# One 512-column matmul over both parts of x in the first layers of three feed-forward blocks, and two pieces of side work moved in a transformer kernel on Trainium2

## The chip, the cores and the metric

The kernel runs on one core of one Trainium2 chip. TensorE (PE in the profile) multiplies, VectorE (DVE), ScalarE (ACT) and GpSimd (POOL) do the element-wise work, SyncE (SP) issues the weight DMAs. The metric is the device time of one execution in microseconds (us). Before the change three runs gave 1234.70, 1237.61 and 1238.38 us, median 1237.61 us.

## The reference

A sequence of 256 tokens with 1024 features goes through two transformer layers and then a third, hybrid block. Everything is float32. Cut to the parts that the change touches:

```python
def sq_relu_mlp(xn, w1, w2):                      # twice, w1: 1024 x 4096
    return jnp.square(jax.nn.relu(xn @ w1)) @ w2

# layer 1: dilated attention; q and k of three groups get rotary tables
q = apply_rope(hcat[:, :, :, 0], cos_f, sin_f)    # [x1*c - x2*s, x2*c + x1*s]
k = apply_rope(hcat[:, :, :, 1], cos_f, sin_f)

# third block: recurrent branch, then a gated feed-forward
xa = causal_dwconv(xa, lru_conv_w[l], lru_conv_b[l])
r = sigmoid(einsum("bshi,hij->bshj", xh, w_a) + b_a)   # i likewise with w_x
g = causal_dwconv(h @ w_ffn_gate[l], ffn_conv_w[l], ffn_conv_b[l])   # 1024 x 3072, 3 taps
x = x + (jax.nn.gelu(g) * (h @ w_ffn_up[l])) @ w_ffn_down[l]
```

## The kernel before

**Products of split operands.** Each float32 weight and activation is held as a high part and a low part (high is the value rounded to TensorE's fp32r format, low the rest). A product is the sum of three matmuls: high by high, low weight by high activation, high weight by low activation. For x the parts are XH and XL, one 128x256 tile for each of 8 chunks of features.

**Weights.** They come as 192 slabs of 1 MB (128 partitions x 2048 numbers), in one fixed order, through five buffers `raw`. ScalarE writes the high part `whi` (three buffers, function `high`, L1118), VectorE subtracts it and writes the low part `wlo` (function `low`, L1558); for some slabs, the gate slabs of the last feed-forward among them, GpSimd does that (L2273). Both are called two slabs ahead of the slab that TensorE works on (`ahead`). `whi` of a slab waits until TensorE has finished the slab three before it.

**A slab of a first layer.** `features` makes 256 output features of 256 tokens: two halves of 128 features (m), 8 chunks, three matmuls of 256 columns each, 48 in all, into the two halves of one PSUM bank. Its order is chunk by chunk, so it needs `wlo` at its second matmul. `features_low_last` (L550) does all 32 matmuls with `whi` first and the 16 with `wlo` behind them. `tokens` and `by_tokens` make token-major values with 256 or 512 moving columns.

**Order.** Nothing is scheduled at run time: the program of each engine is written out by hand as five functions, one for each engine, and semaphores order them against each other. An engine whose next instruction waits stands still, with all that is behind it.

**The two squared-ReLU blocks (`mlp`).** 16 slabs of W1, then 16 of W2. For each W1 slab ScalarE applies Relu from PSUM into TA (L1222), VectorE squares into TB (L1717), ScalarE rounds TB into HH (L1227), VectorE writes the rest into HL (L1722). Two TA and two TB buffers alternate.

**The gated feed-forward.** 12 pairs of slabs, gate and up. For pair j VectorE scales the gate product out of PSUM into `gv` (memory SN, L2180), applies the three taps (L2186, L2192) into TA, ScalarE applies Gelu (L1516), VectorE multiplies with the up product from PSUM into TB (L2200), ScalarE rounds into HH (L1501), VectorE writes HL (L2206).

**Slabs of the dilated attention.** q and k slabs are rotated: ScalarE copies the product into TA (L1376), four DMAs on its own queue (L1382) bring its 32-row groups swapped into TB, GpSimd multiplies that with the sine (L2339), VectorE multiplies the product with the cosine (L1940) and adds the swapped half (L1920, function `rotate`). Ten slabs (EARLY) stand ahead of the attention, the first six of them q and k. The copy of slab k waits until the sum of slab k-2 is done.

**Recurrent gates.** In the third block's 12 input slabs (`IN2`) VectorE makes a causal convolution of four chunks (`conv`, L2039 and L2043), one behind each of slabs 1 to 4. `lru_gate` multiplies them with small per-head matrices (L994) and ScalarE applies Sigmoid (L1413); slabs 6 and 7 are the attention values.

## Time and profile before

| what | value |
|---|---|
| median of 3 runs | 1237.61 us |
| the profiled execution: its time / its span | 1235.95 / 1234.0 us |
| PE busy | 1218.7 us (99%), 8673 matmuls |
| DVE, ACT, POOL busy | 800.3, 631.4, 206.5 us (65%, 51%, 17%) |
| chain that ended last | PE 89%, DVE 6%, ACT 2% |
| matmuls with x: XH by wlo, XH by whi, XL by whi | 1256 of 256 columns each on line 536 |

The profiled execution took 1235.95 us, of which 1234.0 us are the span shown. The engine lines give busy time; a matmul's own duration (284 ns for 256 columns) holds its way through the array, which overlaps the next one, so the distance from start to start is what counts. The chain is followed back from the last instruction to what released it.

### The profile page before, as it was taken

Reading aid. Unit: us, or ns where it says so; the run is one execution under the profiler, and the core shown is the slowest. Engines: PE = TensorE matmul, PEld = TensorE weight load, DVE = VectorE, ACT = ScalarE, POOL = GpSimd, SP = SyncE. Lnnn points to the kernel's source line nnn. Section 1 sums busy time; section 2 is a strip of 40 time slices with the busy share of each in tenths; the row PEclk is TensorE's granted clock in tenths of the full one; section 3 lists DMA queues with packets and bytes.
Section 4 is the critical chain, followed back from the end, with each engine's and each line's share of the span. In section 5 each row is a group of like instructions: output and inputs, shape, how many; then the busy total and the mean of one; then the engine's idle time right before and its main releaser. Section 6 shows DMA issues by size and latency. Waiting matters only on the chain.

```text
span 1234.0 us, 20616 instructions
## 1 busy us (share of the span) xinstructions
PE 1218.7 (99%) x8673; PEld 1118.9 (91%) x8673; DVE 800.3 (65%) x1071; ACT 631.4 (51%) x785; POOL 206.5 (17%) x160
## 2 busy tenths in 40 slices
PE   9999999999999999999999999998999999999998
PEld 8988999988899989999999988897978899999986
DVE  7778666644475665676876754586975477656643
ACT  5574455534454454445655543455576646444442
POOL 2500010000010201210310000010010695443100
PEclk9999999999999999999999999999999999999999
DMA  9733466555566555654355556554554455555551
GB/s 250 243 103 108 138 183 188 173 203 182 194 212 211 176 179 163 190 186 147 103 165 178 182 194 201 175 185 138 184 163 165 139 190 185 188 171 173 199 182 62
DMA packets 162075, 214.32 MB, mean 174 GB/s; under 512 B 5259, under 2 KB 117198, under 8 KB 161982
## 3 DMA queue, kind: packets, MB, share of 16 engines
q1 hardware_dynamic: 156574, 205.11, 51.6%
q10 hardware_dynamic: 5216, 7.42, 2.1%
q8 instruction: 69, 1.13, 0.4%
q0 software_dynamic: 192, 0.46, 0.2%
q14 instruction: 24, 0.20, 0.0%
HBM read 205.63 MB, written 1.05 MB: 167 GB/s over the span
## 4 chain that ended last, share of the span: by engine, by line
PE 89%; DVE 6%; ACT 2%; DMA 1%; issue 1%; SPq 0%; ACTq 0%; POOL 0%; DVEq 0%
PE ps L536 77%; PE ps L705 3%; PE ps L608 3%; PE ps L742 2%; PE ps L713 2%; DVE wlo L1558 2%; DMA raw<-in_ev_w_in_dram 1%; ACT whi L1118 1%; DVE XT L1691 0%; DVE XL L1596 0%; DVE BIG L2043 0%; DMA TB<-TA 0%; ACTq L1382 0%; DVE RS L1591 0%; PE ps L878 0%
## 5 line engine op out<-in xcount | busy, mean ns | idle before, releaser
L1558 DVE TENSOR_TENSOR wlo<-raw,whi 128x2048 fp32r<-128x2048 f32 (+1 forms) x167 | 385.8, 2311 | 224.2 <-ACT whi L1118 224.0
L1118 ACT ACTIVATE whi<-raw 128x2048 fp32r<-128x2048 f32 x188 | 357.8, 1906 | 196.0 <-PE ps L536 179.8
L536 PE MATMUL ps<-XH,wlo 128*128 128x256 f32 x1256 | 349.5, 284 | 2.4 <-DVE wlo L1558 2.2
L536 PE MATMUL ps<-XH,whi 128*128 128x256 f32 x1256 | 351.3, 285 | 0.0
L536 PE MATMUL ps<-XL,whi 128*128 128x256 f32 x1256 | 349.2, 283 | 0.0
L536 PEld LDWEIGHTS ps<-XH,wlo 128*128 128x128 f32 x1256 | 238.6, 192 | 3.1 <-DVE wlo L1558 3.1
L536 PEld LDWEIGHTS ps<-XH,whi 128*128 128x128 f32 x1256 | 238.6, 192 | 0.2
L536 PEld LDWEIGHTS ps<-XL,whi 128*128 128x128 f32 x1256 | 238.5, 192 | 0.0
L536 PE MATMUL ps<-whi,HL 128*128 128x512 f32 (+1 forms) x416 | 148.7, 373 | 0.0
L536 PE MATMUL ps<-whi,HH 128*128 128x512 f32 x384 | 147.2, 390 | 0.0
L536 PE MATMUL ps<-wlo,HH 128*128 128x512 f32 x368 | 143.2, 389 | 0.0
L2273 POOL TENSOR_TENSOR wlo<-raw,whi 128x512 fp32r<-128x512 f32 x88 | 115.3, 1343 | 145.3 <-ACT whi L1118 145.2
L536 PE MATMUL ps<-whi,XH 128*128 128x512 f32 (+1 forms) x288 | 98.2, 349 | 0.0
L2339 POOL TENSOR_TENSOR TB<-TB,BIG 128x512 f32<-128x512 f32 x24 | 36.4, 1516 | 366.7 <-DMA TB<-TA 366.7
L536 PE MATMUL ps<-wlo,XH 128*128 128x512 f32 (+1 forms) x288 | 96.4, 343 | 0.0
L536 PE MATMUL ps<-whi,XL 128*128 128x512 f32 (+1 forms) x288 | 96.3, 342 | 0.0
L536 PEld LDWEIGHTS ps<-whi,HL 128*128 128x128 f32 x416 | 76.0, 188 | 13.5
L1180 ACT ACTIVATE SN<-SN,stat 128x512 f32<-128x512 f32 (+2 forms) x64 | 38.3, 598 | 96.4 <-DVE stat L1630 93.9
L536 PEld LDWEIGHTS ps<-whi,HH 128*128 128x128 f32 x384 | 71.9, 188 | 14.7
L536 PEld LDWEIGHTS ps<-wlo,HH 128*128 128x128 f32 x368 | 69.1, 188 | 14.5
L536 PEld LDWEIGHTS ps<-whi,XH 128*128 128x128 f32 x288 | 53.6, 190 | 6.9 <-issue 1.1
L536 PEld LDWEIGHTS ps<-wlo,XH 128*128 128x128 f32 x288 | 53.6, 189 | 6.5
(271 smaller groups left out, 1758.3 us busy)
## 6 DMA issues: line engine op xcount, KB each, us to landing
raw<-in_mlp_w_dram SPq DMA_DIRECT2D x64, 1024.0 KB, 5.3
raw<-in_od_w_in_dram SPq DMA_DIRECT2D x36, 1024.0 KB, 5.4
raw<-in_w_in_dram SPq DMA_DIRECT2D x24, 1024.0 KB, 5.1
raw<-in_w_ffn_gate_dram SPq DMA_DIRECT2D x12, 1024.0 KB, 5.2
raw<-in_w_ffn_up_dram SPq DMA_DIRECT2D x12, 1024.0 KB, 5.1
raw<-in_w_ffn_down_dram SPq DMA_DIRECT2D x12, 1024.0 KB, 5.0
TB<-TA ACTq DMA_DIRECT2D x96, 64.0 KB, 4.1
raw<-in_w_branch_dram SPq DMA_DIRECT2D x6, 1024.0 KB, 5.0
```

What stands on the lines that cost most here:

```text
L536: m = pe.matmul(to, l[c][a], r[c][b], start=first and k == 0, stop=last and k == 3 * n - 1)
L608: i = pe.matmul(b[n][:, m * S:m * S + S], h[a], x[c][z], start=m == c == a == z == 0, stop=m == 1 and c == 7 and z == 1)
L705: m = pe.matmul(banks[u][:, lo:hi], l, r, start=start, stop=stop)
L713: m = pe.transpose(b[:, to:to + P], SN[:, u % 3, of:of + P], ident[:, :])
L742: m = pe.matmul(b[p0:p0 + n, a:z], v, PT[:, u % 3, lo:hi], start=start, stop=stop)
L1118: act.activation(whi_of(n), raw_of(n), ACT.Copy, scale=1.0).then_inc(*tell(s_whi, ("whi", n)))
L1180: m = act.activation(SN[:, u % 3, lo:hi], src[:, lo:hi], ACT.Exp, bias=stat[:, u % 3, k:k + 1], scale=-1.0 if biased else 1.0, accum_out=s ...
L1558: dve.tensor_tensor(wlo_of(n), raw_of(n), f32(whi_of(n)), ALU.subtract).then_inc(*tell(s_wlo, ("wlo", n)))
L2273: m = pool.tensor_tensor(lo[:, v], r[:, v], f32(hi[:, v]), ALU.subtract)
L2339: pool.tensor_tensor(z, z, twice(RP[:, S:512]), ALU.mult).then_inc(*tell(s_pool, ("sine", k)))
```

## The change

Three things are edited.

**1. Both parts of x beside each other.** XH and XL become two halves of one tile XHL, 512 columns for each chunk. A new function `beside` replaces `features` for slabs 2 to 15 of both squared-ReLU blocks and slabs 2 to 23 of the gated feed-forward, 14 + 14 + 22 = 50 slabs. Per half it does 8 matmuls of `whi` by 512 columns and then 8 of `wlo` by the 256 high columns, into a bank of its own: columns 0 to 255 hold high x and low weight sums, 256 to 511 the part of low x. ScalarE copies the second half of each bank to SBUF (`copies`), VectorE adds the first half to it (`added`); then the ReLU and the square are one VectorE instruction, and the gated feed-forward scales and multiplies from SBUF. In `mlp` VectorE's `low` stands behind the square instead of ahead of it.

```diff
+            def beside(n, x, between=None):
+                for m in range(2):
+                    b = bank(("beside", n, m))
+                    w = w_ready(n, 8, m * P, P)
+                    for c in range(8):
...
+                        pe.matmul(b[:, :], w[c][0], XHL[:, c, :], start=c == 0, stop=False)
+                    for c in range(8):
+                        once.wait_ge(*at(w[c][3]))
+                        i = pe.matmul(b[:, 0:S], w[c][1], x[c][0], start=False, stop=c == 7)
...
-                    features(W1[layer] + j, x_ready(f"mlp{layer}"))
+                    beside(W1[layer] + j, x_ready(f"mlp{layer}"))
...
-                features(n, x)
+                beside(n, x)
...
+            def copies(n, to, *ready):
+                for m in range(2):
+                    b = take(("beside", n, m), ready)
+                    act.activation(to[:, m * S:m * S + S], b[:, S:2 * S], ACT.Copy, scale=1.0)...
...
+            def added(n, to, copy):
+                for m in range(2):
+                    b = take(("beside", n, m), [("copy", n, m)])
+                    v = slice(m * S, m * S + S)
+                    dve.tensor_tensor(to[:, v], b[:, 0:S], copy[:, v], ALU.add)...
+                once.wait_ge(*at(("taken", "beside", n, 1)))
...
+                        added(W1[layer] + j, a, z)
+                        dve.scalar_tensor_tensor(out=z, in0=a, scalar=0.0, in1=a, op0=ALU.max, op1=ALU.mult)...
...
+                if j:
+                    copies(FF + 2 * j, TA[j % 2], *([("ffn z", j - 2)] if j > 1 else []))
                 once.wait_ge(*at(("ffn conv", j)))
                 act.activation(TA[j % 2][:, :], TA[j % 2][:, :], ACT.Gelu_apprx_tanh)...
+                if j:
+                    copies(FF + 2 * j + 1, TB[j % 2], *([("hlo", 2, j - 2)] if j > 1 else []))
```

**2. Swapped halves' sums moved back.** Among the first ten dilated slabs the sum of the swapped half stands two slabs behind its own, behind the `low` of that slab, and slabs 4 and 5 also use `features_low_last`.

```diff
-                        (features_low_last if i < 4 else features)(n, x)
+                        (features_low_last if i < 6 else features)(n, x)
...
+                rotate(1)
...
-                rotate()
-                pending[0] = hb, g, w, rotated[0]
+                if i >= EARLY:
+                    rotate(0)
+                pending.append((hb, g, w, rotated[0]))
```

**3. Recurrent gates moved back.** `lru_gate` runs behind input slabs 6 and 7 instead of 5 and 6, on TensorE and ScalarE; the steps that follow it (Tanh, Exp, `lru_ratio`) move back by one slab with it.

```diff
-                if n in (5, 6):
-                    lru_gate(n - 5)
+                if n in (6, 7):
+                    lru_gate(n - 6)
```

What now stands in the rows of three engines follows. L1558 of before is L1591 of the changed kernel (`low`), L1940 is L1986 (cosine), L1920 is L1965 (swapped half's sum).

VectorE, first dilated slabs. Before:

```order
L1940 TENSOR_TENSOR BIG<-ps,BIG 128x512 x2
L1920 TENSOR_TENSOR BIG<-BIG,TB 128x512
L1558 TENSOR_TENSOR wlo<-raw,whi 128x2048
L1940 TENSOR_TENSOR BIG<-ps,BIG 128x512
L1920 TENSOR_TENSOR BIG<-BIG,TB 128x512
```

And changed:

```order
L1986 TENSOR_TENSOR BIG<-ps,BIG 128x512 x2
L1591 TENSOR_TENSOR wlo<-raw,whi 128x2048
L1965 TENSOR_TENSOR BIG<-BIG,TB 128x512
L1986 TENSOR_TENSOR BIG<-ps,BIG 128x512
L1591 TENSOR_TENSOR wlo<-raw,whi 128x2048
```

The low part of slab 4's weights now stands ahead of the first sum of a swapped half, which waits for DMAs and GpSimd.

TensorE, third block, input slab 5 and what follows. Before:

```order
L550 MATMUL ps<-XH,whi 128x256
L550 MATMUL ps<-XL,whi 128x256
L550 MATMUL ps<-XH,wlo 128x256 x16
L994 MATMUL ps<-BIG,SN 64x256 x8
L536 MATMUL ps<-whi,XH 128x512
L536 MATMUL ps<-whi,XL 128x512
L536 MATMUL ps<-wlo,XH 128x512
```

And changed (L570 is `features_low_last`, L538 the product, L1014 the gate):

```order
L570 MATMUL ps<-XHL,whi 128x256 x32
L570 MATMUL ps<-XHL,wlo 128x256 x16
L538 MATMUL ps<-whi,XHL 128x512 x2
L538 MATMUL ps<-wlo,XHL 128x512
...
L1014 MATMUL ps<-BIG,SN 64x256 x8
```

The 24 matmuls of slab 6 now stand between slab 5 and the first gate.

VectorE, one pair of the gated feed-forward, from its gate scaling to the next. Before:

```order
L2180 TENSOR_TENSOR SN<-ps,RS 128x512
L2186 TENSOR_SCALAR TA<-SN,FV 128x256 x2
L2192 SCALAR_TENSOR_TENSOR TA<-SN,FV,TA 128x255 x2
L2192 SCALAR_TENSOR_TENSOR TA<-SN,FV,TA 128x254 x2
L1558 TENSOR_TENSOR wlo<-raw,whi 128x2048
L2206 TENSOR_TENSOR HL<-TB,HH 128x512
L2200 TENSOR_TENSOR TB<-TA,ps 128x512
```

And changed:

```order
L1718 TENSOR_TENSOR SN<-ps,TA 128x256 x2
L2228 TENSOR_TENSOR SN<-SN,RS 128x512
L2238 TENSOR_SCALAR TA<-SN,FV 128x256 x2
L2244 SCALAR_TENSOR_TENSOR TA<-SN,FV,TA 128x255 x2
L2244 SCALAR_TENSOR_TENSOR TA<-SN,FV,TA 128x254 x2
L1591 TENSOR_TENSOR wlo<-raw,whi 128x2048
L2261 TENSOR_TENSOR HL<-TB,HH 128x512
L1718 TENSOR_TENSOR TB<-ps,TB 128x256 x2
L2252 TENSOR_TENSOR TB<-TA,TB 128x512
```

Four additions of 256 columns have come in, two ahead of the scaling and two ahead of the multiplication.

ScalarE, one pair of the gated feed-forward, from its Gelu on. Before:

```order
L1516 ACTIVATE TA<-TA 128x512
L1118 ACTIVATE whi<-raw 128x2048
L1501 ACTIVATE HH<-TB 128x512
L1118 ACTIVATE whi<-raw 128x2048
L1513 ACTIVATE BIG<-ps 128x2x256
```

And changed (L1197 is `copies`, L1547 the Gelu, L1138 `high`, L1530 HH, L1542 a copy that four of the pairs have):

```order
L1547 ACTIVATE TA<-TA 128x512
L1197 ACTIVATE TB<-ps 128x256 x2
L1138 ACTIVATE whi<-raw 128x2048
L1530 ACTIVATE HH<-TB 128x512
L1138 ACTIVATE whi<-raw 128x2048
L1542 ACTIVATE BIG<-ps 128x2x256
L1197 ACTIVATE TA<-ps 128x256 x2
```

The copies of the gate product stand behind the second `whi` of the pair, which stands behind HH.

## Rows read from the trace of the kernel before

**Rows 1.** The page: span, engines busy (share, instructions).
```profile
span 1234.0 us, 20616 instructions
PE 1218.7 (99%) x8673; PEld 1118.9 (91%) x8673; DVE 800.3 (65%) x1071; ACT 631.4 (51%) x785; POOL 206.5 (17%) x160
```

**Rows 2.** Waits of PE: in total, times, longest.
```profile
PE ps L994 <- DVE BIG L2043: 3.5, 1, 3.5
PE ps L536 <- DVE wlo L1558: 2.2, 1, 2.2
```

**Rows 3.** Windows: length, busy time (count) of PE, PEld, DVE, ACT, POOL, clock, DMA.
```profile
360.10:363.60 3.50, 3.48 (x17) 3.49 (x18) 2.60 (x3) 1.50 (x3) 1.28 (x1) 0.54 0.88 283
```

**Rows 4.** Timeline of VectorE, first dilated slabs: start, length, what.
```profile
352.02 1.29 DVE L1940 TENSOR_TENSOR BIG<-ps,BIG 128x512 f32<-128x512 f32 x2
357.17 0.69 DVE L1920 TENSOR_TENSOR BIG<-BIG,TB 128x512 f32<-128x512 f32 x1 [3.86 <-POOL TB L2339]
357.77 2.29 DVE L1558 TENSOR_TENSOR wlo<-raw,whi 128x2048 fp32r<-128x2048 f32 x1
```

**Rows 5.** Timeline of ScalarE, same stretch.
```profile
352.43 1.90 ACT L1118 ACTIVATE whi<-raw 128x2048 fp32r<-128x2048 f32 x1
```

**Rows 6.** Chain of waits, same stretch.
```profile
351.28 4.49 DMA TB<-TA
355.84 1.30 POOL TB L2339
```

**Rows 7.** Timeline of PE, ahead of and in the first recurrent gate.
```profile
837.79 1.51 PE L994 MATMUL ps<-BIG,SN 64*64 64x256 f32 x12
842.82 0.65 PE L994 MATMUL ps<-BIG,SN 64*64 64x256 f32 x4 [3.52 <-DVE BIG L2043]
```

**Rows 8.** Chain of waits, a stretch of 256 columns, one of 512.
```profile
1052.08 23.03 PE ps L536 x192
300.37 32.66 PE ps L536 x144
```

**Rows 9.** Groups by line and shape, whole span: count, busy, mean ns, idle before.
```profile
L1717 DVE TENSOR_TENSOR TB<-TA 128x512 f32<-128x512 f32 x32 | 21.9, 685 | 1.2 <-ACT TA L1222 1.2
L1663 DVE TENSOR_TENSOR OL<-ps,OH 128x256 fp32r<-128x256 f32 x16 | 6.8, 424 | 28.9 <-ACT OH L1198 28.9
L1691 DVE TENSOR_TENSOR XT<-XT,ps 128x256 f32<-128x256 f32 x32 | 17.8, 599 | 1.2 <-PE ps L536 1.1
L2227 DVE SCALAR_TENSOR_TENSOR BIG<-ps,RS,BIG 128x512 f32<-128x512 f32 x4 | 3.0, 748 | 9.4 <-PE ps L536 9.3
L1198 ACT ACTIVATE OH<-ps 128x256 fp32r<-128x256 f32 x16 | 6.1, 384 | 1.5 <-PE ps L742 1.5
L1170 ACT ACTIVATE BIG<-ps,RS 128x256 f32<-128x256 f32 x4 | 1.7, 481 | 0.1
```

**Rows 10.** Timeline of VectorE, one pair of the gated feed-forward.
```profile
1087.09 0.69 DVE L2180 TENSOR_TENSOR SN<-ps,RS 128x512 f32<-128x512 f32 x1 [4.88 <-PE ps L536]
1087.82 1.10 DVE L2186 TENSOR_SCALAR TA<-SN,FV 128x256 f32<-128x256 f32 x2
1088.95 1.79 DVE L2192 SCALAR_TENSOR_TENSOR TA<-SN,FV,TA 128x255 f32<-128x255 f32 x4
1090.66 2.29 DVE L1558 TENSOR_TENSOR wlo<-raw,whi 128x2048 fp32r<-128x2048 f32 x1
1092.86 0.69 DVE L2206 TENSOR_TENSOR HL<-TB,HH 128x512 fp32r<-128x512 f32 x1
1093.46 0.68 DVE L2200 TENSOR_TENSOR TB<-TA,ps 128x512 f32<-128x512 f32 x1
```

**Rows 11.** Timeline of ScalarE, same pair.
```profile
1087.09 1.91 ACT L1118 ACTIVATE whi<-raw 128x2048 fp32r<-128x2048 f32 x1 [3.33 <-PE ps L536]
1088.91 0.58 ACT L1513 ACTIVATE BIG<-ps 128x512 f32<-128x512 f32 x1
```

**Rows 12.** Weight loads of PE in the first squared-ReLU block, by shape.
```profile
L536 PEld LDWEIGHTS ps<-XH,wlo 128*128 128x128 f32 x224 | 43.0, 192 | 0.0
```

More of the change, by code:

```diff
@@ L1220, in mlp @@
                         ahead(W1[layer] + 1)
-                    b = take(("slab", W1[layer] + j), [("hlo", layer, j - 2)] if j > 1 else ())
-                    act.activation(TA[j % 2][:, :], b[:, :], ACT.Relu).then_inc(
-                        *tell(s_act_out, ("taken", "slab", W1[layer] + j), ("relu", layer, j)))
+                    if j < 2:
+                        b = take(("slab", W1[layer] + j))
+                        act.activation(TA[j % 2][:, :], b[:, :], ACT.Relu).then_inc(
+                            *tell(s_act_out, ("taken", "slab", W1[layer] + j), ("relu", layer, j)))
+                    else:
+                        copies(W1[layer] + j, TB[j % 2], ("hlo", layer, j - 2))
                     if j == 0:
@@ L1703, in mlp @@
                 for j in range(16):
-                    if not 1 <= j <= 2:
-                        ahead(W1[layer] + j)
                     if j == 0:
+                        ahead(W1[layer])
                         ahead(W1[layer] + 1)
@@ L1715, in mlp @@
                     a, z = TA[j % 2][:, :], TB[j % 2][:, :]
[L1716 to L1717 removed]
+                    if j < 2:
+                        once.wait_ge(*at(("relu", layer, j)))
+                        dve.tensor_tensor(z, a, a, ALU.mult).then_inc(*tell(s_dve, ("h", layer, j)))
+                    else:
+                        added(W1[layer] + j, a, z)
+                        dve.scalar_tensor_tensor(out=z, in0=a, scalar=0.0, in1=a, op0=ALU.max, op1=ALU.mult).then_inc(
+                            *tell(s_dve, ("h", layer, j)))
                     if j == 0:
                         ahead(W1[layer] + 2)
+                    if j > 2:
+                        ahead(W1[layer] + j)
                     once.wait_ge(*at(("h", layer, j)))
@@ L2178, in ffn_conv @@
                 y, s0 = pair(TA[j % 2][:, :]), pair(gv[j % 2])
-                b = take(("slab", FF + 2 * j))
-                dve.tensor_tensor(s0, pair(b[:, :]), twice(r6), ALU.mult).then_inc(*tell(s_dve_out, ("taken", "slab", FF + 2 * j)))
-                once.wait_ge(*at(("taken", "slab", FF + 2 * j)))
+                if j:
+                    added(FF + 2 * j, gv[j % 2], TA[j % 2])
+                    dve.tensor_tensor(s0, s0, twice(r6), ALU.mult).then_inc(*tell(s_dve, ("ffn s", j)))
+                    once.wait_ge(*at(("ffn s", j)))
+                else:
+                    b = take(("slab", FF))
+                    dve.tensor_tensor(s0, pair(b[:, :]), twice(r6), ALU.mult).then_inc(*tell(s_dve_out, ("taken", "slab", FF)))
+                    once.wait_ge(*at(("taken", "slab", FF)))
                 if j > 1:
```

62 lines of the change are left out of this document (35 added, 27 removed).

## The prediction
> **What bounds the kernel now.** I read the page first: TensorE is busy for 1218.7 of 1234.0 us, no other engine above 65% [rows 1]. So the time is the number of matmuls by their distance, plus TensorE's few waits. The waits come next. After the start-up only two are over 1 us: 3.5 us for the convolution ahead of the first recurrent gate and 2.2 us for a low weight part [rows 2]. The windows show what the second drags behind it: for the 3.5 us after that pause the granted clock was 0.54, so about half, the 1.2 GHz level, and 17 matmuls were begun where some 29 fit [rows 3]. Last come the distances. 192 matmuls of 256 columns took 23.03 us, 0.1199 us each; 144 of 512 took 32.66 us, 0.2268 us each [rows 8]. Twice the columns cost 0.1069 us more, so each matmul carries 0.1199 - 0.1069 = 0.0130 us that do not depend on its columns.
>
> **Part 1, 50 slabs in the new form.** A slab was 48 matmuls of 256 columns, 48 x 0.1199 = 5.755 us. Now it is 16 of 512 and 16 of 256: 16 x 0.2268 + 16 x 0.1199 = 5.547 us. The columns are the same; 16 matmuls' fixed parts go, 0.208 us a slab. 50 slabs: 10.4 us. These sums are distances, so all of it lies on TensorE's own path, if nobody else becomes late. The trace has 512 and 256 columns only in stretches of one kind; a mixed row is bounded by the plain ones: below by no fixed part left at all (another 32 x 0.013 = 0.4 us a slab), above by the 192 ns of a weight load [rows 12] behind each wide matmul. I take the plain distances, since 192-ns loads already hide behind 120-ns matmuls.
>
> What it adds elsewhere. ScalarE gets copies of 256 columns out of PSUM; the nearest rows are 384 ns (plain scale) and 481 ns (scale from SBUF) [rows 9]; these have the plain scale, so 0.38. VectorE gets additions of 256 columns with one operand in PSUM: 424 ns for such a shape, 599 ns in the row with a strided target [rows 9]; these are contiguous, so 0.42. The new square does ReLU and product in one: 0.69 like the old square, at most the 0.75 of the row with three inputs [rows 9].
>
> In the squared-ReLU blocks VectorE then does per slab: low part 2.20 (start to start [rows 10]), HL 0.60, two additions 0.84, square 0.69: 4.33 of 5.55 us. The longest loop between the engines is square 0.69, HH some 0.6, `whi` 1.82 [rows 11], two copies 0.76, second addition 0.42: 4.3 us. Both fit, so TensorE hides all of it. The Relu on ScalarE goes, two copies come.
>
> The gated feed-forward is tight. ScalarE's order ties a loop through the whole pair: multiply 0.68, HH about 0.62, second `whi` 1.82, two copies 0.76, second addition 0.42, then VectorE's scaling 0.73, first tap 1.13, other taps 1.71, low part 2.20, HL 0.60 [rows 10, 11], two additions 0.84. Sum 11.5 us; with each instruction's last 0.1 us overlapped where nothing waits for it, 11.4. TensorE needs 2 x 5.55 = 11.1 us a pair, and 11.3 with the four groups of transposes spread over eleven pairs. So this chain slips by 0.1 to 0.4 us a pair. What it can slip: before, the low part of an up slab was done at 1092.95 and its slab began 11.52 us after 1087.09, at 1098.61, 5.7 us later [rows 10]. Now `wlo` is first needed 8 x 0.227 = 1.8 us into the slab, the pair is 0.4 us shorter, and the taps start some 3.1 us later (behind `whi` 1.9, two copies, an addition): 5.7 + 1.8 - 0.4 - 3.1 = 4.0 us. Ten pairs slip by 1 to 4 us, so I count no stall, with little to spare. What is late behind the last pair, HH and HL of pair 11, is first needed five slabs of 5.4 us later.
>
> **Part 2, the swapped halves.** Before, VectorE stood 3.86 us for GpSimd ahead of the first sum, and the low part behind it began at 357.77 [rows 4]; the sum hangs on ScalarE's DMAs, 4.49 us to land, and GpSimd's 1.30 us [rows 6]. Now the low part goes first: `whi` is there at 354.33 [rows 5], so `wlo` at 356.65, before TensorE gets to that slab at 357.9, and with the low matmuls last it would have 3.8 us more. The wait of 2.2 us goes, and so does the slow stretch behind it: 3.5 us at 0.54, worth 3.5 x 0.46 = 1.6 us. Together 3.8 us. What is late next: the sums wait behind low parts, and the copies on ScalarE behind the sums. Going through slabs 5 to 9 with these durations, each low part ends 0.5 to 2.3 us ahead of the matmul that needs it; the closest is slab 9's, queued behind the two last sums (second sine ready at about 383.1, low part done at 386.0, needed at 386.5). I take no stall; up to 1 us may come there. Four DMAs of each slab on ScalarE's queue are as before, only later by up to some 2 us.
>
> The Trainium skill (TensorE: Matmul & The Clock Gate, "Back-to-back issue gap") has for a single warm matmul a gap of N / 2.4 + 2.5 ns. The measured 119.9 and 226.8 ns [rows 8] are 10.7 ns above it at both widths, so the trace does not agree. By the page's fixed part each slab would save 16 x 2.5 = 40 ns, the 50 slabs 2.0 us instead of 10.4.
>
> **Part 3, the recurrent gates.** TensorE stood 3.52 us for the fourth chunk's convolution [rows 7]. Now slab 6 comes first, 24 matmuls of 512 columns, 24 x 0.2268 = 5.4 us [rows 8], whose weights were ready by VectorE's order (its low part stands two slabs earlier than the convolution's end). 5.4 covers 3.5, so 3.5 us go, and no slow clock hung on this pause. Tanh, Exp and the ratio move back one slab, 5.8 us later, with three slabs and some attention steps still ahead of their use: nothing on TensorE's path.
>
> **Sum.** 10.4 + 3.8 + 3.5 = 17.7 us. The profiled execution: 1234.0 [rows 1] - 17.7 = 1216.3 span, with its 1.95 us outside 1218.3. It was 1.7 us below the median of the runs shown, so against that median 1219.9. I say 1219.5.
>
> **Rivals.**
> *The feed-forward loop becomes the bound.* For it: 11.4 against 11.3 us. If an addition takes the 599 ns of the strided row and a copy 481 ns, the loop gains three additions by 0.18 and two copies by 0.1, 0.7 us a pair; over ten pairs 7 us and the 1 to 4 of slip, less the 4.0 in hand: 4 to 7, by a pair-by-pair walk 5.4 us. Time 1225. Against: the contiguous rows say 0.42. Sign: TensorE waiting for L1591 from pair 5 or so on. 11%.
> *Side work moves the waits instead of removing them.* If slab 9's low part or a gate's Sigmoid delays TensorE and the clock drops again, up to 1.5 + 2 us of parts 2 and 3 stay. Time 1223. 9%.
> *The fixed part does not belong to the matmul's count.* If the 13 ns come with changing weights between x parts and stay per column, part 1 brings 2.0 us or less. Time 1237.6 - 2.0 - 7.3 = 1228. Against: 0.1199 and 0.2268 fit one constant at both widths. 5%.
> *Slower: the mixed widths break the overlap of weight loads.* In the new slabs a 256-column matmul stands at times behind a wide one, and both write one bank. If a low matmul waited for its 192-ns load instead of hiding it, it would cost 0.072 us more, 16 x 50 x 0.072 = 58 us: 1277. The change is undone from 17.7 / 800 = 0.022 us per wide and narrow pair on, that is when the two take over 0.369 us together. Against: loads of 192 ns sit behind 120-ns matmuls everywhere [rows 12]. 4%.
> My forecast with its own range of 1216 to 1223: 71%.
>
> **Numbers.** The range runs from 1215.5 (a bit more fixed part saved) to 1227 (the loop bites fully). About 0.3%, 3.7 us, is what can be told from no change. All cases but the last are faster by more; of the last, most is slower, and a small share of mild cases lands near zero. Faster 0.93, same 0.03, slower 0.04.
>
> **What would show it.** Slabs of 5.55 us (32 matmuls) in the three blocks; no PE wait for L1591 near 355 and no stretch of half clock there; no wait of the gate on the convolution near 825; in the gated feed-forward VectorE idle under 1 us a pair, its low part ending later each pair against TensorE, and TensorE still without a gap. PE's count falls by 800. I am wrong if the wide and narrow pair takes other than 0.347 us, or if TensorE waits in pairs 5 to 11.

## The result and the profile after

The changed kernel takes 1230.57 us (median of 4 runs, 1230.0 to 1231.61), the kernel before 1237.58 beside it: ratio 0.9949, 95% interval 0.9931 to 0.9966. It is 7.0 us faster. 17.7 us and a time of 1219.5 were forecast, at most 1227, so the time lies outside the range. The profiled execution is 5.7 us shorter, 1228.3 against 1234.0 [rows 1]. Its page:

```profile
span 1228.3 us, 19289 instructions
PE 1212.6 (99%) x7873; PEld 1076.4 (88%) x7873; DVE 834.8 (68%) x1171; ACT 643.1 (52%) x857; POOL 210.2 (17%) x160
```

TensorE has exactly 800 matmuls fewer. Lay the same landmarks of both traces side by side (the first matmul of each block) and the gain builds up in steps: -0.3 us at the start, -2.4 over the first squared-ReLU block, -3.6 over the dilated slabs, -2.2 over the second block, -3.8 over the recurrent gates. Before the gated feed-forward the changed kernel is 12.1 us ahead. From there to the end it loses 6.5: 1.1 in the first layers of that block, which take 141.9 us instead of 140.8, and 5.4 from the last product on, 76.7 us instead of 71.4. TensorE's waits, after (engine, line waited in, releaser: us in total, times, longest):

```profile
PE ps L538 <- DVE wlo L1591: 3.7, 1, 3.7
PE ps L556 <- POOL wlo L2328: 2.8, 6, 0.6
PE ps L850 <- DVE ones L1788: 1.0, 1, 1.0
```

The two waits of [rows 2] are gone, and two new kinds stand in their place, both in the gated feed-forward: six short ones for GpSimd's low part, one long one for VectorE's. (The wait on line 850 is in the start-up and was there before.) The windows of that block (stretch: length, then busy us of PE, PEld, DVE, ACT, POOL, then clock). One of the kernel before:

```profile
1100.00:1120.00 20.00, 20.00 (x169) 20.00 (x168) 12.56 (x19) 9.06 (x9) 6.69 (x6) 1.00 0.60 197
```

And of the changed one:

```profile
1100.00:1120.00 20.00, 19.00 (x108) 16.07 (x107) 13.52 (x23) 9.42 (x13) 10.82 (x8) 1.00 0.59 193
1140.00:1160.00 20.00, 17.04 (x89) 14.05 (x87) 15.28 (x25) 8.29 (x14) 2.07 (x2) 1.00 0.55 179
...
1161.00:1164.40 3.40, 3.08 (x7) 2.48 (x8) 2.60 (x6) 1.11 (x2) 0.00 (x0) 0.51 0.16 62
```

PE, 20.00 of 20 us in the windows of this block before, is short by 0.6 to 3.0 us in each 20 from 1080 on, and the last row is a stretch at the 1.2 GHz level. What TensorE does around it (timeline of PE: start, us, operation, and in brackets idle before and releaser):

```profile
1148.76 2.00 PE L553 MATMUL ps<-XHL,whi 128*128 128x512 f32 x8
1150.60 1.11 PE L556 MATMUL ps<-XHL,wlo 128*128 128x256 f32 x8
1151.55 0.40 PE L538 MATMUL ps<-whi,HH 128*128 128x512 f32 x1
...
1157.25 0.39 PE L538 MATMUL ps<-whi,HL 128*128 128x512 f32 x1
1161.32 0.79 PE L538 MATMUL ps<-wlo,HH 128*128 128x512 f32 x1 [3.68 <-DVE wlo L1591]
1161.91 0.63 PE L538 MATMUL ps<-whi,HH 128*128 128x512 f32 x1
...
1164.40 0.39 PE L538 MATMUL ps<-whi,HH 128*128 128x512 f32 x1
```

Three readings. A half slab in the new form takes 1151.55 - 1148.76 = 2.79 us (1148.76 to 1150.60, 1.84, for eight wide matmuls, 0.95 for eight narrow ones), a slab 5.59 (two halves of 2.793 on average), not 5.55. The second slab of the last product pauses for its low part. And behind the pause seven matmuls take 3.08 us where 0.23 each would be 1.6, so the pause costs some 1.5 us more.

Now the pair of slabs ahead of that pause, on VectorE (L1718 addition, L2228 scaling, L2238 and L2244 taps, L1591 low part, L2261 HL, L2252 the product z of Gelu and up):

```profile
1130.13 0.69 DVE L2228 TENSOR_TENSOR SN<-SN,RS 128x512 f32<-128x512 f32 x1
...
1136.92 1.49 DVE L2252 TENSOR_TENSOR TB<-TA,TB 128x512 f32<-128x512 f32 x1
1141.25 0.76 DVE L1718 TENSOR_TENSOR SN<-ps,TA 128x256 f32<-128x256 f32 x2 [2.84 <-ACT TA L1197]
1142.04 0.69 DVE L2228 TENSOR_TENSOR SN<-SN,RS 128x512 f32<-128x512 f32 x1
...
1148.45 2.29 DVE L1591 TENSOR_TENSOR wlo<-raw,whi 128x2048 fp32r<-128x2048 f32 x1 [0.32 <-ACT whi L1138]
1150.66 0.75 DVE L1718 TENSOR_TENSOR TB<-ps,TB 128x256 f32<-128x256 f32 x2
1151.45 0.69 DVE L2252 TENSOR_TENSOR TB<-TA,TB 128x512 f32<-128x512 f32 x1
1154.98 0.76 DVE L1718 TENSOR_TENSOR SN<-ps,TA 128x256 f32<-128x256 f32 x2 [2.84 <-ACT TA L1197]
...
1158.98 2.28 DVE L1591 TENSOR_TENSOR wlo<-raw,whi 128x2048 fp32r<-128x2048 f32 x1
```

ScalarE and GpSimd in the same pair:

```profile
1134.52 1.92 ACT L1138 ACTIVATE whi<-raw 128x2048 fp32r<-128x2048 f32 x1
1138.45 0.63 ACT L1530 ACTIVATE HH<-TB 128x512 fp32r<-128x512 f32 x1 [2.01 <-DVE TB L2252]
1138.98 1.90 ACT L1138 ACTIVATE whi<-raw 128x2048 fp32r<-128x2048 f32 x1
1140.79 0.63 ACT L1197 ACTIVATE TA<-ps 128x256 f32<-128x256 f32 x2
```

```profile
1136.58 5.49 POOL L2328 TENSOR_TENSOR wlo<-raw,whi 128x512 fp32r<-128x512 f32 x4 [6.91 <-ACT whi L1138]
```

From scaling to scaling the loop takes 1142.04 - 1130.13 = 11.91 us here, and 12.4 in the four pairs with a rows copy (L1542), where 11.4 were forecast against 11.1 to 11.3 for TensorE. At its measured price TensorE needs 2 x 5.59 = 11.2 us, and 11.6 where a group of transposes stands between (they added 0.43 us in the kernel before, 11.95 for 11.52 from scaling to scaling). The loop runs VectorE's z, ScalarE's HH, `whi`, copies, VectorE's addition, and from there VectorE's own row down to the next z. In these pairs no member of it waits for TensorE. GpSimd hangs on it too: it writes the low part of a gate slab as soon as the pair's first `whi` (1134.52 above) is there, which stands behind the Gelu and the up copies, so when the loop falls behind, those low parts come late, and they are what TensorE waits for. z takes 1.49 us instead of 0.68 [rows 10]: it starts 0.34 us behind the start of a GpSimd instruction and both read two tensors from SBUF. VectorE stands idle 2.84 us for the copies behind `whi`. The last pair also holds a second low part (1148.45), that of the first slab of the last product, and z of pair 10 waits behind it; the next low part, at 1158.98, is the one that TensorE pauses for.

Parts 2 and 3 went as forecast. VectorE at the first swapped sum, after:

```profile
351.76 2.29 DVE L1591 TENSOR_TENSOR wlo<-raw,whi 128x2048 fp32r<-128x2048 f32 x1 [1.13 <-ACT whi L1138]
355.24 0.69 DVE L1965 TENSOR_TENSOR BIG<-BIG,TB 128x512 f32<-128x512 f32 x1 [1.19 <-POOL TB L2394]
```

The low part goes first and the sum waits 1.19 us instead of 3.86 [rows 4]. The recurrent gate starts at 834.58 without a gap, where [rows 7] show 3.52 us of standing still.

### The profile page after: what moved, and what is told of

Same layout as the page of the kernel before. It is cut to its first block, busy times and chain, and to the rows that moved or that the text cites. A ratio compares the mean times of both kernels' runs of the same rounds, so it can differ in the third digit from the quotient of the medians.

```text
span 1228.3 us, 19289 instructions
## 1 busy us (share of the span) xinstructions
PE 1212.6 (99%) x7873; PEld 1076.4 (88%) x7873; DVE 834.8 (68%) x1171; ACT 643.1 (52%) x857; POOL 210.2 (17%) x160
## 3 DMA queue, kind: packets, MB, share of 16 engines
q8 instruction: 62, 1.02, 0.4%
## 4 chain that ended last, share of the span: by engine, by line
PE 81%; DVE 9%; ACT 5%; issue 4%; DMA 0%; POOL 0%; ACTq 0%; DVEq 0%
PE ps L538 50%; PE ps L553 8%; PE ps L556 4%; PE ps L628 4%; PE ps L570 4%; ACT whi L1138 3%; PE ps L725 3%; PE ps L762 2%; PE ps L733 2%; DVE TA L2244 1%; DVE wlo L1591 1%; DVE TB L2252 1%; PE ps L594 1%; DVE TA L2238 1%; DVE SN L2228 1%
## 5 line engine op out<-in xcount | busy, mean ns | idle before, releaser
L1591 DVE TENSOR_TENSOR wlo<-raw,whi 128x2048 fp32r<-128x2048 f32 (+1 forms) x167 | 385.0, 2308 | 188.1 <-ACT whi L1138 187.8
L1138 ACT ACTIVATE whi<-raw 128x2048 fp32r<-128x2048 f32 x188 | 357.8, 1906 | 151.8 <-PE ps L538 132.8
L553 PE MATMUL ps<-XHL,whi 128*128 128x512 f32 x800 | 200.9, 393 | 0.0
L553 PEld LDWEIGHTS ps<-XHL,whi 128*128 128x128 f32 x800 | 143.8, 189 | 25.8
L538 PE MATMUL ps<-XHL,whi 128*128 128x256 f32 x848 | 153.0, 285 | 0.0
L538 PE MATMUL ps<-whi,HL 128*128 128x512 f32 (+1 forms) x416 | 149.2, 374 | 0.0
L538 PE MATMUL ps<-whi,HH 128*128 128x512 f32 x384 | 147.7, 391 | 0.0
L538 PE MATMUL ps<-wlo,HH 128*128 128x512 f32 x368 | 144.0, 391 | 3.7 <-DVE wlo L1591 3.7
L538 PE MATMUL ps<-whi,XHL 128*128 128x512 f32 (+1 forms) x576 | 145.2, 345 | 0.0
L2328 POOL TENSOR_TENSOR wlo<-raw,whi 128x512 fp32r<-128x512 f32 x88 | 118.8, 1381 | 147.4 <-ACT whi L1138 147.1
L538 PEld LDWEIGHTS ps<-XHL,whi 128*128 128x128 f32 x848 | 130.5, 191 | 0.6 <-issue 0.4
L556 PEld LDWEIGHTS ps<-XHL,wlo 128*128 128x128 f32 x800 | 108.5, 190 | 13.9 <-POOL wlo L2328 5.4
L556 PE MATMUL ps<-XHL,wlo 128*128 128x256 f32 x800 | 112.3, 283 | 3.3 <-POOL wlo L2328 2.8
L538 PE MATMUL ps<-XHL,wlo 128*128 128x256 f32 x424 | 113.2, 283 | 0.0
L538 PEld LDWEIGHTS ps<-whi,XHL 128*128 128x128 f32 x576 | 97.8, 190 | 12.3 <-issue 0.7
L538 PE MATMUL ps<-wlo,XHL 128*128 128x512 f32 (+1 forms) x288 | 96.4, 343 | 0.0
L538 PEld LDWEIGHTS ps<-whi,HL 128*128 128x128 f32 x416 | 76.3, 189 | 13.7
L538 PEld LDWEIGHTS ps<-wlo,HH 128*128 128x128 f32 x368 | 69.5, 189 | 18.8 <-DVE wlo L1591 4.1
L538 PEld LDWEIGHTS ps<-whi,HH 128*128 128x128 f32 x384 | 72.4, 189 | 14.8
L538 PEld LDWEIGHTS ps<-XHL,wlo 128*128 128x128 f32 x424 | 78.2, 192 | 0.2 <-DVE wlo L1591 0.2
```

The costliest lines, as they stand in the source:

```text
L538: m = pe.matmul(to, l[c][a], r[c][b], start=first and k == 0, stop=last and k == 3 * n - 1)
L553: pe.matmul(b[:, :], w[c][0], XHL[:, c, :], start=c == 0, stop=False)
L556: i = pe.matmul(b[:, 0:S], w[c][1], x[c][0], start=False, stop=c == 7)
L1138: act.activation(whi_of(n), raw_of(n), ACT.Copy, scale=1.0).then_inc(*tell(s_whi, ("whi", n)))
L1591: dve.tensor_tensor(wlo_of(n), raw_of(n), f32(whi_of(n)), ALU.subtract).then_inc(*tell(s_wlo, ("wlo", n)))
L2328: m = pool.tensor_tensor(lo[:, v], r[:, v], f32(hi[:, v]), ALU.subtract)
```

## The experiments

The theory: the wide form gains wherever it stands, and the gated feed-forward turns the gain into a loss because the loop z, HH, `whi`, copies, addition is longer than TensorE's pair. The rivals: part 1 gains nothing anywhere; GpSimd's low part stretches VectorE, and that alone is the loss; VectorE simply has too much work. The letters in the quoted expectations are explained in each of them. A time "in spans" compares profiled executions, one for each kernel; "in medians" compares all runs. In the code cuts "..." stands for lines left out.

**The moves alone** (parts 2 and 3; part 1 undone):

```diff
-                    beside(W1[layer] + j, x_ready(f"mlp{layer}"))
+                    features(W1[layer] + j, x_ready(f"mlp{layer}"))
...
-                beside(n, x)          # gated feed-forward
+                features(n, x)
...
-                    added(FF + 2 * j, gv[j % 2], TA[j % 2])
```

> Parts 2 and 3 alone (swapped halves' sums and recurrent gates moved back; all first layers as before, 256-column matmuls). Theory A (the moved waits go, each worth what it cost before): 3.6 + 3.7 us less than before, about 1230.3 us. Rival B (part of what the changed kernel gained there hangs on the new slabs ahead of them): under 5 us less, above 1232.5 us.

1228.19 us (1227.39 to 1228.99), ratio 0.9927 [0.9912, 0.9941]. The moves are worth 9.3 us in medians, 7.4 in the spans of the profiled executions (1226.6 against 1234.0); 7.3 were forecast. So all of part 1 together costs 2.4 us net in medians, 1.7 in spans. The 1.9 us between the two figures for the moves look like clock, though no profile shows it: the runs of the kernel before have a mean granted clock of 0.995 or 0.996, its profiled execution 0.997, and one more stretch of 3.4 us at half clock is 1.7 us and 0.0014 of the mean. The profile of before has no such stretch behind the recurrent gate's pause; the run with part 1 alone, below, has one.

**The gated feed-forward as before**, parts 2 and 3 and the squared-ReLU blocks changed:

```diff
-                beside(n, x)
+                features(n, x)
...
-                    added(FF + 2 * j, gv[j % 2], TA[j % 2])
+                b = take(("slab", FF + 2 * j))
```

> The changed kernel with its gated feed-forward as before; both squared-ReLU blocks keep the wide matmuls. Theory A (the loop between ScalarE and VectorE through one pair bounds the gated feed-forward, which costs about 6.5 us net there): the feed-forward's part of the loss goes, some 6.5 us under the changed kernel, about 1224.5 us, no TensorE wait over 1 us after 40 us. Rival B (the loss sits elsewhere, e.g. the denser squared-ReLU blocks): within 2 us of the changed kernel's 1230.6.

1225.00 us (1223.37 to 1226.04), ratio 0.9904 [0.9887, 0.992]. The 28 slabs gain 3.2 us in medians (5.0 in spans; 28 x 0.17 = 4.7 by the slab's length), and the 22 of the gated feed-forward cost 5.6 (6.7 in spans). That rules out that part 1 gains nowhere, and puts the loss where the landmarks do.

**Part 1 alone** (the moves undone, `pending` and the gates' place as in the kernel before):

```diff
-                        (features_low_last if i < 6 else features)(n, x)
+                        (features_low_last if i < 4 else features)(n, x)
...
-                if n in (6, 7):
-                    lru_gate(n - 6)
+                if n in (5, 6):
+                    lru_gate(n - 5)
...
-                if i >= EARLY:
-                    rotate(0)
+                rotate(0)
```

> Part 1 alone as the changed kernel has it (swapped halves' sums and recurrent gates where they were before). Theory A (the three parts add up: the moves are worth 7.3 to 9.3 us, the wide form 4.6 in the squared-ReLU blocks, and the gated feed-forward costs 6.5): 2 us over the kernel before at most, 1236 to 1240 us, so no gain from the wide form by itself as it is ordered. Rival B (the moves and the wide form hang on each other): under 1234 us.

1239.74 us (1237.18 to 1241.89, 10 runs), ratio 1.0022 [1.0012, 1.0031]: as written, part 1 by itself makes the kernel a little slower. That is 2.5 us over the kernel before beside it (1237.28). Added to the moves' -9.3 it makes -6.8, about the -7.0 of both together. Its waits:

```profile
PE ps L538 <- DVE wlo L1591: 6.5, 2, 3.7
PE ps L1014 <- DVE BIG L2088: 3.5, 1, 3.5
PE ps L556 <- POOL wlo L2326: 2.8, 6, 0.6
```

Both old waits are back beside both new ones, and the clock fell to the lower level for 3.4 us behind each of the three long pauses, the recurrent gate's among them. In the profile of the kernel before that one had no such stretch behind it.

**ScalarE's copies ahead of the second `whi`** of a pair:

```diff
                     ffn_high(j - 1)
+                if j:
+                    copies(FF + 2 * j, TA[j % 2], *([("ffn z", j - 2)] if j > 1 else []))
                 ahead(FF + 2 * j + 1)
...
-                if j:
-                    copies(FF + 2 * j, TA[j % 2], *([("ffn z", j - 2)] if j > 1 else []))
```

> The changed kernel with one move on ScalarE: the two copies of the gate product stand ahead of the pair's second whi instead of behind it. Theory A (the loop HH, second whi, copies, taps, low part, additions, product of 11.9 us a pair is the bound): the 1.8 us of whi leave the loop, it takes 10.1 us, under TensorE's 11.3; all TensorE waits of the feed-forward go, about 10 us less than the changed kernel, 1220 to 1221 us. Rival B (GpSimd's low parts, 5.5 us each against 5.1 before, are late because they are slow and start late by themselves): the waits at the gate slabs stay at 0.4 to 0.7 us each, under 5 us gained, above 1225 us.

1222.16 us (1221.16 to 1223.9), ratio 0.9879 [0.9865, 0.9894]: 8.4 us under the changed kernel, by a change of order alone. VectorE and ScalarE in the pair:

```profile
1130.29 1.50 DVE L2252 TENSOR_TENSOR TB<-TA,TB 128x512 f32<-128x512 f32 x1
1132.82 0.76 DVE L1718 TENSOR_TENSOR SN<-ps,TA 128x256 f32<-128x256 f32 x2 [1.04 <-ACT TA L1197]
1133.61 1.14 DVE L2228 TENSOR_TENSOR SN<-SN,RS 128x512 f32<-128x512 f32 x1
1134.79 1.59 DVE L2238 TENSOR_SCALAR TA<-SN,FV 128x256 f32<-128x256 f32 x2
```

```profile
1131.82 0.63 ACT L1530 ACTIVATE HH<-TB 128x512 fp32r<-128x512 f32 x1 [2.02 <-DVE TB L2252]
1132.36 0.64 ACT L1197 ACTIVATE TA<-ps 128x256 f32<-128x256 f32 x2
1132.88 1.92 ACT L1138 ACTIVATE whi<-raw 128x2048 fp32r<-128x2048 f32 x1
```

z is still 1.50, scaling and tap are stretched as well (1.14 and 1.59 against 0.69 and 0.74), and yet TensorE has no wait at a gate slab: 20.00 of 20 us busy in each window from 1080 to 1140, as here:

```profile
1100.00:1120.00 20.00, 20.00 (x118) 17.64 (x117) 18.64 (x26) 9.98 (x14) 9.08 (x7) 1.00 0.52 170
```

The first layers of the block take 137.1 us, 3.7 less than in the kernel before: 22 slabs by 0.17, all of the gain of the wide form. Taking 1.8 us of `whi` out of the loop was enough. The theory of the loop holds; that the stretched instructions alone are the loss, or VectorE's amount of work, does not (VectorE is busier here in the same window, 18.64 us against 13.52). Two things went otherwise than expected. The loop takes 11.4 us, not 10.1, because VectorE now meets GpSimd on scaling and tap too and loses 1.3 of the 1.8 us there; that is no more than TensorE's own mean of 11.4, so it is just enough. And only 4.8 of the 8.9 us in spans come from these layers; 4.1 come from the last product on, where the pause shrinks from 3.7 to 1.0 us and no half clock follows it. Whether the loop would have fitted without the stretched instructions and with the copies where they were is not shown: in the next runs the stretch only changes its place.

**GpSimd's low part behind z**:

```diff
             for n in range(FF, SLABS):
+                if n < FD and (n - FF) % 2 == 0 and n > FF:
+                    once.wait_ge(*at(("ffn z", (n - FF) // 2 - 1)))
                 ahead(n)
```

> The changed kernel, but GpSimd starts each low part of a gate slab only when VectorE's product (Gelu times up) of the pair before is done. Theory C (the product of two SBUF operands takes 1.50 instead of 0.69 us because GpSimd starts at the same time, and that 0.8 us is part of the loop): the product takes 0.69 us, the loop 11.1 instead of 11.9 us; GpSimd begins 0.3 us later and TensorE's waits shrink; 4 to 9 us less than the changed kernel, 1222 to 1227. Rival D (the 1.5 us has another cause): the product keeps 1.5 us, GpSimd starts 1.8 us later, and the waits grow: above 1232 us.

1230.66 us (1230.17 to 1234.19), ratio 0.9953 [0.9937, 0.9968]: no change, which neither side of the expectation had. VectorE, then GpSimd:

```profile
1099.64 0.69 DVE L2252 TENSOR_TENSOR TB<-TA,TB 128x512 f32<-128x512 f32 x1
1104.45 1.57 DVE L2228 TENSOR_TENSOR SN<-SN,RS 128x512 f32<-128x512 f32 x1
```

```profile
1100.41 5.06 POOL L2328 TENSOR_TENSOR wlo<-raw,whi 128x512 fp32r<-128x512 f32 x4 [6.57 <-DVE TB L2252]
```

The contention is real: z is 0.69 again. But 0.9 us comes back on the scaling 5 us later (in every second pair on the tap instead), in the same loop, which takes 12.0 and 12.5 us as against 11.9 and 12.4, and GpSimd is later too (waits of 4.8 us for it in place of 2.8). The collision was moved, not removed.

**GpSimd's instruction cut in eight, and in two** (256 and 1024 columns instead of 512):

```diff
-                for q in range(4):
-                    v = slice(512 * q, 512 * q + 512)
+                for q in range(8):
+                    v = slice(256 * q, 256 * q + 256)
```

> The changed kernel with GpSimd's low part of a slab in eight instructions of 256 columns instead of four of 512. Theory C (VectorE's product of two SBUF operands stands until GpSimd's running instruction ends, so the 0.8 us is the rest of one 1.2-us instruction): the product takes about 1.0 instead of 1.50 us, the loop of a pair 11.4 instead of 11.9, TensorE's waits shrink by a half or more unless eight instructions take GpSimd clearly longer than 5.5 us; 1225 to 1229 us. Rival D (the product is slow because both engines share bandwidth during all of it): 1.5 us as before, no change from 1230.6.

> The changed kernel with GpSimd's low part in two instructions of 1024 columns. Theory C (VectorE waits for the end of the running GpSimd instruction): the product takes 0.7 plus about 2.1 us, 2.8 us, the loop 13.2 us a pair, well over TensorE's 11.3; 10 to 15 us more than the changed kernel, 1240 to 1246 us. Rival D (shared bandwidth): 1.5 us and 1230.6 us as before.

1235.79 us (1234.69 to 1238.38, 8 runs), ratio 0.9993 [0.9983, 1.0004], and 1248.34 us (1247.14 to 1249.53), ratio 1.0093 [1.0071, 1.0114]. z and the GpSimd work beside it, in eighths:

```profile
1105.61 0.94 DVE L2252 TENSOR_TENSOR TB<-TA,TB 128x512 f32<-128x512 f32 x1
...
1105.26 6.06 POOL L2328 TENSOR_TENSOR wlo<-raw,whi 128x256 fp32r<-128x256 f32 x8 [5.46 <-ACT whi L1138]
```

In halves:

```profile
1102.01 2.60 DVE L2252 TENSOR_TENSOR TB<-TA,TB 128x512 f32<-128x512 f32 x1
...
1101.67 5.21 POOL L2328 TENSOR_TENSOR wlo<-raw,whi 128x1024 fp32r<-128x1024 f32 x2 [8.30 <-ACT whi L1138]
```

The same z, started 0.34 to 0.35 us behind a GpSimd instruction, takes 0.94, 1.49 and 2.60 us as that instruction has 256, 512 and 1024 columns. The running GpSimd instruction takes 0.74, 1.29 and 2.39 us, and z ends 0.55 us behind its end in all three: it stands until the running one is through. Shared bandwidth, the rival, would not follow the size of the pieces.

Both times came out above what was expected. In halves the loop grows by another 1.1 us and the kernel falls behind the one before; its profile also has the longer dilated stretch that the next run shows (2.8 us) and a pause of 2.8 us at 990 with half clock behind it, so not all of the 17.8 us is the loop. In eighths z gains 0.55 us, but scaling (1.02 or 1.22 us) and tap meet GpSimd more often and the loop is as long as before; GpSimd needs 6.1 to 6.5 us for a slab instead of 5.5, and a wait of 2.7 us appears in the attention part, with half clock behind it. The profiles side by side, in us (a pair is from scaling to scaling, without and with a rows copy; in the kernel before it is TensorE's pace, without and with transposes):

| kernel | a pair | first layers of the block | last product to the end |
|---|---|---|---|
| before | 11.5, 11.95 | 140.8 | 71.4 |
| changed | 11.9, 12.4 | 141.9 | 76.7 |
| copies first | 11.4, 11.4 | 137.1 | 72.6 |
| GpSimd behind z | 12.0, 12.5 | 143.7 | 76.0 |
| GpSimd in eighths | 11.9, 12.5 | 143.2 | 76.0 |
| GpSimd in halves | 13.0, 13.5 | 151.4 | 77.0 |

**The last pair.** On top of the copies first, `ahead(FD)` goes ahead of HH and HL of pair 11 on ScalarE and VectorE:

```diff
+            ahead(FD)
             ffn_high(11)
...
-            for k in range(6):
+            for k in range(1, 6):
```

> Copies first (as in the kernel with the gate copies ahead of the second whi), and besides the high and low part of the third slab of the down product stand ahead of HH and HL of the last pair. Theory A (the remaining TensorE wait of 1.0 us at 1158 us is for that slab's low part, which queues behind the last pair's product, HH and HL): the wait goes, 1 us less than copies first, about 1221.1 us. Rival B (the next low part is late in its place): no change, 1222.2 us, with a wait of like size one or two slabs later.

1221.69 us (1218.9 to 1222.62), ratio 0.9874 [0.9857, 0.989]. The wait of 1.0 us that the copies-first kernel had left at 1159 is gone, and from the last product on it takes 71.4 us instead of 72.6, but the medians differ by 0.5 us only, within their spread: inconclusive in time. Its profile shows something else, beside the dilated slabs (VectorE, then GpSimd's sine product):

```profile
367.05 1.78 DVE L1966 TENSOR_TENSOR BIG<-BIG,TB 128x512 f32<-128x512 f32 x1
```

```profile
366.92 1.36 POOL L2396 TENSOR_TENSOR TB<-TB,BIG 128x512 f32<-128x512 f32 x1 [2.37 <-DMA TB<-TA]
```

The same two engines again: the sum meets the sine product, takes 1.78 us, and TensorE then loses 0.6 to 1.2 us three times. Of ten profiled kernels with the moves (the code there is the same), three have this (this one, the next, and the one in halves) and need 2.5 to 2.8 us more for the stretch. The sine product starts when its DMAs have landed, so this looks like a matter of their timing in a run; it was not taken apart further.

**Wide and narrow in turn**, first everywhere (on the copies first), then (on the last pair's order) in the squared-ReLU blocks only from slab 4 on. The edit of the first:

```diff
                         pe.matmul(b[:, :], w[c][0], XHL[:, c, :], start=c == 0, stop=False)
-                    for c in range(8):
                         once.wait_ge(*at(w[c][3]))
```

> Copies first, with the 16 matmuls of a half in the order wide, narrow, wide, narrow instead of eight wide and then eight narrow. In the changed kernel the first five wide matmuls of a half start 228 to 236 ns apart and the last three 227. Theory A (wide matmuls that follow a run of narrow ones pay while weight loads catch up, about 50 ns a half): interleaving makes the pair 0.347 us, 2.773 us a half instead of 2.793, or some 2 us less in all, about 1220. Rival B (each change from one width to the other costs): 8 changes a half instead of one, halves of 2.85 us and more, 1226 us or above.

> Copies first and last weights (1221.7 us), with wide and narrow matmuls in turn in slabs 4 to 15 of the squared-ReLU blocks and in the gated feed-forward; slabs 2 and 3 keep the low matmuls last. Theory A (a half takes 2.776 instead of 2.793 us in turn, and the full version lost only by waits of the first slabs, where the low part is needed 1.8 us earlier): 24 + 22 slabs by 0.034 us, 1.6 us less, about 1220.1 us, no wait over 0.5 us in these slabs. Rival B (the low parts are needed too early in the gated feed-forward too): waits for L1592 or GpSimd there, 1222 us or more.

1224.69 us (1223.58 to 1228.31), ratio 0.9907 [0.9884, 0.993], and 1224.5 us (1220.82 to 1225.89), ratio 0.9901 [0.9885, 0.9918]. Both were expected at 1220 us. Alternating, a pair is 230 + 117 = 347 ns in many slabs, 2.77 us for a half slab, the sum of the prediction; in blocks of eight the eight wide ones take 1.84 us and the eight narrow ones 0.95, 2.79 together. But other alternating halves take 2.82 to 2.83 us, the wide ones 0.236 each, among them about half of those of the gated feed-forward, whose first layers then take 137.3 and 137.7 us against 137.1 in blocks of eight. So no gain is shown there; which halves are slow was not explained. And `wlo` is now wanted at the second matmul, and both runs pay a 2 us wait in the second block for it; the first also has the longer dilated stretch. In the profiled execution of the second (1220.82 us) the clock did not fall behind that wait. Its three other runs, of 1223.4 to 1225.9 us, have a lower mean clock, 0.997 or 0.998 against 0.999. Neither order shows the 1277 us of the rival with mixed widths.

**The first six swapped sums on GpSimd** (on the run before), so that VectorE cannot meet the sine product; then, on top, alternating only from slab 6 on. The edits of the two:

```diff
+                if i < 6:
...
+                    pool.tensor_tensor(dst, dst, TB[k % 2][:, :], ALU.add)...
```

```diff
-                    beside(W1[layer] + j, x_ready(f"mlp{layer}"), mixed=j > 3)
+                    beside(W1[layer] + j, x_ready(f"mlp{layer}"), mixed=j > 5)
```

> As the kernel with mixed matmuls, and the six sums of swapped halves ahead of the dilated attention are done by GpSimd behind its own product, not by VectorE. In the profiles so far that stretch takes 69.9 to 70.5 us or 72.4 to 72.7; in the long ones VectorE's sum takes 1.78 instead of 0.69 us, beside a GpSimd product. Theory C (VectorE's sum of two SBUF operands waits for the running GpSimd instruction, which tips the chain of copies over 5.76 us a slab): with no such sum on VectorE the stretch takes 69.9 us in the profile, and the median is 0 to 1.5 us lower. Rival D (the long stretches come from the DMAs of the swapped halves): it can take 72.5 us as before, and GpSimd's own sums of some 1.3 us lengthen the chain, so 1 us or more over the kernel with mixed matmuls.

> This is the run before it (copies first, last pair's parts first, the first six swapped sums on GpSimd) with one number changed: the wide and the narrow matmuls alternate in the squared-ReLU blocks only from slab 6 on (before: from slab 4 on), and in the whole gated feed-forward as before. Theory A (the wait of 2.06 us at 641 was slab 5's low part, which VectorE writes beside slab 3 and which an alternating slab needs at its second matmul): the wait and the slower stretch behind it (3.4 us at half clock, some 1.7 us) go, about 3 us less in the profile and 1222.6 - 3 + some 0.1 for the two plain slabs: 1220. Rival B (VectorE is simply late there and any slab would wait): the wait moves to slab 7, time as before, 1222.6. Rival C (the run-to-run difference of some 2.8 us in the stretch of the dilated slabs is larger than the rest): median anywhere from 1219 to 1223, with no wait over 1 us in the second block.

1222.62 us (1221.67 to 1224.57), ratio 0.9884 [0.987, 0.9899], and 1221.89 us (1220.62 to 1222.61), ratio 0.9876 [0.9858, 0.9895]. The dilated stretch is the short one in both, as it was in the run before; so these two do not contradict the collision as its cause, but cannot prove it. In the first, slab 5's low part is written at

```profile
640.91 2.29 DVE L1595 TENSOR_TENSOR wlo<-raw,whi 128x2048 fp32r<-128x2048 f32 x1
```

and TensorE loses 2.05 us for it, with 3.4 us of half clock behind. In the second that wait is gone; the largest that stay (of 1.0 us and below) are those of every version:

```profile
PE ps L853 <- DVE ones L1792: 1.0, 1, 1.0
PE ps L631 <- DVE XHL L1633: 0.5, 1, 0.5
```

The span fell by 1.8 us, the median by 0.7, where 2.6 were expected of it. The four best versions (medians 1221.7 to 1222.6) cannot be told apart; all beat the changed kernel by some 8 to 9 us, and almost all of that is the copies' place (8.4 us).

## Why the prediction was wrong

*Part 1, the price of a slab.* The mechanism held: 16 fewer matmuls a slab save time at the same number of columns. The size was off: 0.17 us a slab, not 0.208, because the wide ones in a mixed slab start 0.230 us apart, not 0.2268. That is 28 x 0.04 = 1.1 us in the squared-ReLU blocks and 0.9 in the other: 2 of the 12.0 us missing between the profiled executions (17.7 forecast, 5.7 measured). The VectorE and ScalarE loop there had room, as forecast.

*Part 1, the gated feed-forward: "so I count no stall".* This is the step that failed, and 4.6 us of gain became a loss of 6.5. The loop was counted at 11.4 us and takes 11.9 to 12.4. The place had been named as a rival (11%, 1225 us), with the wrong reasons: additions and copies cost what was forecast (0.42 and 0.37 each). Its sign was half right, since TensorE waits from pair 6 on, mostly for GpSimd's line and not for L1591. Four other things were missing.
1. z. The sum took 0.68 us from a row where its second operand came from PSUM. After the change both are in SBUF, and it takes 1.49 beside GpSimd's low part. The trace of before had the sign of it: L2186 at 1.10 us in [rows 10], which is 0.74 where GpSimd is idle. I carried 1.10 as that line's own cost. In the changed kernel this tap meets nobody and takes 0.77, so 0.81 us too little for z and 0.36 too much for the tap make the 0.5 us between 11.4 and 11.9.
2. The rows copy of 0.6 us on ScalarE [rows 11], in the loop of four of the pairs, was left out of the sum; it makes their 12.4.
3. The loop itself: with these the pair is 11.9 to 12.4 us, some 0.8 over TensorE's 11.2 to 11.6, and what was in hand (4.0 us by the forecast) is used up by pair 6. From there the six gate slabs get their low parts 0.4 to 0.8 us late, 3.8 us in all. The trace shows two more pieces: the first low matmul behind each such wait takes 0.22 us instead of 0.11, and the up slab of pair 10 waits 0.3 us for VectorE's low part (1135.67), 1.0 us together.
4. The end. I wrote that what is late behind the last pair "is first needed five slabs later", true of HH and HL; but the low parts of the last product's first two slabs stand in or behind the same queue and are needed at once. 3.8 us of pause, and 1.5 us of half clock behind it.
3.8 + 1.0 + 3.8 + 1.5 = 10.1 us, and 0.9 for the slab's price: 11.0 of the 11.1 between -4.6 and +6.5.

*The chance of no stall.* A sum of 11.4 against 11.3 with eleven terms taken from other instructions' rows says nothing about the sign of the difference. The 71% rested on it, and on 4.0 us in hand, when one term off by 0.4 us a pair uses those up within ten pairs.

*Parts 2 and 3.* Right in mechanism and size: -3.6 and -3.8 us by the landmarks, -3.8 and -3.5 forecast. The clock stretch of [rows 3] went with its pause. "No slow clock hung on this pause" was true of the one profile read; the run with part 1 alone has such a stretch behind the same pause, so part 3 may be worth up to 1.7 us more in other executions than the 3.5 forecast, which would fit the 9.3 us of the moves in medians. "Up to 1 us may come there" was too small: in three of ten profiles it is 2.5 to 2.8 us, again through a VectorE sum beside GpSimd.

*The rivals.* The fixed part does belong to the count of matmuls (a slab does save 0.17 us), so 1228 was near the time for a wrong reason. The argument against it was weak, though: any two distances fit one constant and one slope. The slab's measured 5.59 us is the better evidence. Mixed widths cost 0.02 us a half slab, not 0.072 us a matmul. One reading is slightly off: by the rule of the Trainium skill quoted there, 226.8 ns lie 11.0 ns above it, not 10.7, which changes nothing else.

*VectorE idle under 1 us a pair* was wrong too, and a pointer: it stands 2.84 us a pair. An engine that is in the bound and yet idle shows that the loop runs through another engine's queue; here that was `whi` standing ahead of the copies.

On z the Trainium skill (SBUF — State Buffer, "Who interferes with whom") says that a VectorE instruction with two SBUF inputs contends with a GpSimd instruction that reads SBUF, and calls the port pair that the two engines share an exclusive lock. This case agrees, with 0.94, 1.49 and 2.60 us for 256, 512 and 1024 columns, and z always ending 0.55 us behind the running instruction. The page bore on this change, and the prediction did not use it.

## What to carry to other kernels

When a stage's work moves to several engines, walk the loop that runs through all their queues, instruction by instruction in queue order, and count what merely stands between two links of it (here 1.8 us of `whi` between HH and the copies); if the loop is within a few per cent of the bound, first look for an instruction that can leave it, since that decides more than any price. Price an edited instruction by a row with the same sources as well as the same shape: an operand moved from PSUM to SBUF can double its time beside GpSimd. Do not expect to win such a collision back by shifting it within the same loop: two runs here did, and the loop stayed as long. And check the hand-over to the next stage separately: slack gathered in a loop is spent there.
